# Sample differential attention: four heads on one 128-column array pass, or on four 32-column strips

## The reference, cut to what matters

```python
s = jnp.einsum('bqhcd,bshcd->bhcqs', q, k) * HEAD_DIM ** -0.5      # b: 8 batches, q: 16 frames, s: 528 keys
s = s + bias; s = where(visible, s, -inf)
p = softmax(s, axis=-1)
p = p[:, :, 0] - lam * p[:, :, 1]                                  # the two halves of a head
o = jnp.einsum('bhqs,bshv->bqhv', p, v)                            # v: 128 wide
o = _rmsnorm(o, g_subln) * (1.0 - lam_init)
```

## Time and profile before

| | |
|---|---|
| runs shown | 2597.21, 2597.66, 2604.88 us; median 2597.66 us |
| the profiled execution | 2597.61 us, of which the span from the first to the last instruction is 2595.2 us |
| PE busy | 2503.7 us (96% of the span), mean granted clock 0.986 |
| DVE, ACT, POOL busy | 1447.8 us (56%), 1033.3 us (40%), 266.0 us (10%) |
| chain that ended last | PE 81%, DVE 8%, issue 4%, ACT 3%, DMA 3% |

### The profile page before, as it was taken

How to read it: one execution, slowest core, us unless ns; L and a number is a source line. 1 busy time by engine, 2 the same in 40 slices (tenths; PEclk the granted TensorE clock), 3 DMA queues, 4 the chain that set the end, 5 groups by cost and what they waited for, 6 DMA issues and landing times.

```text
span 2595.2 us, 36227 instructions
## 1 busy us (share of the span) xinstructions
PE 2503.7 (96%) x13547; PEld 2155.1 (83%) x13547; DVE 1447.8 (56%) x2884; ACT 1033.3 (40%) x1801; POOL 266.0 (10%) x363
## 2 busy tenths in 40 slices
PE   7999999999989999999999999999999999999998
PEld 5999999878867677778778889989888889888887
DVE  4534444454355358887655348888876545444444
ACT  3322222233332136566424337777565523222221
POOL 1100000014200001110014300000100001000000
PEclk7999999999999999999999999999999999999999
DMA  6212121233355253333433462232311132322221
GB/s 223 82 66 82 66 82 65 102 126 119 109 160 168 68 174 95 112 106 92 160 114 102 149 190 70 85 98 77 98 53 45 49 139 68 135 98 97 98 91 71
DMA packets 169004, 271.29 MB, mean 105 GB/s; under 512 B 72096, under 2 KB 104384, under 8 KB 168832
## 3 DMA queue, kind: packets, MB, share of 16 engines
q0 software_dynamic: 43200, 167.29, 19.2%
q1 hardware_dynamic: 125632, 101.69, 12.3%
HBM read 235.21 MB, written 35.29 MB: 104 GB/s over the span
## 4 chain that ended last, share of the span: by engine, by line
PE 81%; DVE 8%; issue 4%; ACT 3%; DMA 3%; SPq 1%; DVEq 0%; ACTq 0%; POOL 0%
PE bank L1383 12%; PE bank L1384 12%; PE bank L1385 12%; PE bank L1400 6%; PE bank L1401 6%; PE bank L1402 6%; PE bank L1420 4%; PE bank L1422 4%; PE bank L1421 4%; PE bank L1510 3%; DVE w_lo L1971 2%; PE bank L1479 1%; PE bank L1645 1%; PE bank L1493 1%; PE bank L1480 1%
## 5 line engine op out<-in xcount | busy, mean ns | idle before, releaser
L1971 DVE TENSOR_TENSOR w_lo<-raw,w_hi 128x1024 fp32r<-128x1024 f32 x320 | 385.9, 1217 | 148.5 <-ACT w_hi L1685 148.0
L1383 PE MATMUL bank<-XTh_a,w_hi 128*128 128x320 f32 x1408 | 441.4, 313 | 7.2 <-DVE w_lo L1971 2.9
L1385 PE MATMUL bank<-XTh_a,w_lo 128*128 128x320 f32 x1408 | 436.9, 310 | 0.0
L1384 PE MATMUL bank<-XTl_a,w_hi 128*128 128x320 f32 x1408 | 436.9, 310 | 0.0
L1685 ACT ACTIVATE w_hi<-raw 128x1024 fp32r<-128x1024 f32 x320 | 331.5, 1047 | 229.2 <-PE bank L1422 127.3
L1400 PE MATMUL bank<-w_hi,hid_hi 128*128 128x512 f32 x792 | 317.4, 401 | 23.0 <-DVE X_b L2002 8.2
L1401 PE MATMUL bank<-w_lo,hid_hi 128*128 128x512 f32 x792 | 313.1, 395 | 0.0
L1402 PE MATMUL bank<-w_hi,hid_lo 128*128 128x512 f32 x792 | 311.1, 393 | 0.0
L1383 PE MATMUL bank<-XTh_b,w_hi 128*128 128x512 f32 x704 | 284.1, 404 | 0.0
L1384 PE MATMUL bank<-XTl_b,w_hi 128*128 128x512 f32 x704 | 279.0, 396 | 0.0
L1385 PE MATMUL bank<-XTh_b,w_lo 128*128 128x512 f32 x704 | 278.9, 396 | 0.0
(11 more groups left out here) (318 smaller groups left out, 4053.7 us busy)
## 6 DMA issues: line engine op xcount, KB each, us to landing
raw<-in_w_gate POOLq DMA_DIRECT2D x44, 1024.0 KB, 5.7
raw<-in_w_up POOLq DMA_DIRECT2D x44, 1024.0 KB, 5.7
raw<-in_w_down POOLq DMA_DIRECT2D x44, 1024.0 KB, 5.3
raw<-in_w_in POOLq DMA_DIRECT2D x16, 1024.0 KB, 5.4
s_k_in<-in_cache_diff_k SPq DMA_DIRECT2D x16, 512.0 KB, 3.8
s_v_in<-in_cache_diff_v SPq DMA_DIRECT2D x8, 1024.0 KB, 5.6
raw<-in_w_out POOLq DMA_DIRECT2D x8, 1024.0 KB, 5.4
q_rows_b<-q_scr SPq DMA_DIRECT2D x80, 64.0 KB, 2.1
```

Of the source, the lines that this page charges most:

```text
L1383: pe.matmul(out, hi[:, k], XTh[g][:, k, lo:up], start=(k == 0), stop=False)
L1384: pe.matmul(out, hi[:, k], XTl[g][:, k, lo:up], start=False, stop=False)
L1385: last = pe.matmul(out, low[:, k], XTh[g][:, k, lo:up], start=False, stop=(k == KD - 1))
L1971: dve.tensor_tensor(hilo(w_lo, u)[:, :, 0:width_of(u)], raw_part(u), hilo(w_hi, u)[:, :, 0:width_of(u)].bitcast(F32), ALU.subtract).then_i ...
```

## The change

The four heads get strips of 32 array columns, and with them 32 output partitions each. In `x_score` a head's stationary operand is only its own 32 columns of `qm` (now 128 columns wide, without the zero blocks), and its output is partitions `h*32` to `h*32+31`; the heads no longer add into one another. The values' matmuls take 32 columns of `s_pT` (16 queries and 16 columns that are zeroed once), write partitions `h*32` on, and the loop runs over key blocks outside and heads inside. ACT's copies into `s_pT` put each head's 16 columns at `h*32`; DVE copies 128 partitions x 128 columns in place of 16 x 512; the store of a batch is four transfers of 16 rows x 128 columns in place of one; the counts on its semaphore go with it.

```diff
--- before.py
+++ after.py
@@ -151,6 +151,7 @@
 ROUNDS = -(-SAMPLE_TOPK // 8)
 KT = PAST // P
 BATCH_PAIRS = DEC_BATCH // 2
+STRIP = P // DIFF_HEADS
 TAGS = ("n1a", "n1b", "n2a", "n2b", "n3a", "n3b")
 
 
@@ -1071,8 +1072,8 @@
                     idx_T = lay_i("s_idx_T", [P, 2, SAMPLE_KEYS])
                 v_in = lay_d("s_v_in", [P, 2, KT + 1, 512])
                 diff_T = lay_d("s_diff_T", [P, 2, DIFF_HEADS, SAMPLE_KEYS])
-                qm = lay_d("s_qm", [P, 2, 640])
-                o_batch = lay_d("s_o_batch", [DEC_SEQ, 2, 512])
+                qm = lay_d("s_qm", [P, 2, P])
+                o_batch = lay_d("s_o_batch", [P, 2, VD])
             with ExitStack() as stage:
                 def lay_e(name, shape, dt=F32):
                     return stage.enter_context(nc.sbuf_tensor(name, shape, dt))
@@ -1599,8 +1600,8 @@
                         part, cols = out_of(key)[:, 0:HALF], slice(n * HALF, (n + 1) * HALF)
                         if diff:
                             for h in range(DIFF_HEADS):
-                                last = pe.matmul(part, qm[:, b % 2, h * P:(h + 1) * P], diff_T[:, b % 2, h, cols], start=(h == 0),
-                                                 stop=(n == 0 and h == DIFF_HEADS - 1))
+                                last = pe.matmul(part[h * STRIP:(h + 1) * STRIP], qm[:, b % 2, h * STRIP:(h + 1) * STRIP],
+                                                 diff_T[:, b % 2, h, cols], start=True, stop=(n == 0))
                         else:
                             half = slice((b % 2) * HD, (b % 2 + 1) * HD)
                             pe.matmul(part, qd[half, b, :], dsa_T[half, (b // 2) % 2, cols], start=True, stop=False)
@@ -1639,11 +1640,11 @@
                     vacant(pe, key)
                     if diff:
                         pe.wait_ge(s_v_loaded[b % 2], 32 * (b // 2 + 1))
-                        for h in range(DIFF_HEADS):
-                            for k in range(KT + 1):
-                                part = slice(0, P if k < KT else DEC_SEQ)
-                                last = pe.matmul(out_of(key)[0:DEC_SEQ, h * VD:(h + 1) * VD],
-                                                 s_pT[part, u % 2, k, h * DEC_SEQ:(h + 1) * DEC_SEQ],
+                        for k in range(KT + 1):
+                            part = slice(0, P if k < KT else DEC_SEQ)
+                            for h in range(DIFF_HEADS):
+                                last = pe.matmul(out_of(key)[h * STRIP:(h + 1) * STRIP, 0:VD],
+                                                 s_pT[part, u % 2, k, h * STRIP:(h + 1) * STRIP],
                                                  v_in[part, b % 2, k, h * VD:(h + 1) * VD], start=(k == 0), stop=(k == KT))
                     else:
                         pe.wait_ge(s_dv_loaded[b % 4], 32 * (b // 4 + 1))
@@ -1934,15 +1935,19 @@
                     if u >= 2:
                         done(act, ("x_weigh", u - 2))
                     done(act, main)
-                    copied = act.activation(s_pT[:, u % 2, 0:KT, 0:width], out_of(main)[:, 0:KT * width].rearrange("p (k n) -> p k n", k=KT), ACT.Copy)
                     if diff:
-                        tail, key = out_of(main)[0:DEC_SEQ, KT * width:(KT + 1) * width], main
+                        if u < 2:
+                            act.wait_ge(s_zeroed, 2 + 1)
+                        strips = s_pT[:, u % 2].rearrange("p k (h n) -> p k h n", n=STRIP)
+                        src = out_of(main)[:, 0:(KT + 1) * width].rearrange("p (k h i) -> p k h i", k=KT + 1, i=DEC_SEQ)
+                        act.activation(strips[:, 0:KT, :, 0:DEC_SEQ], src[:, 0:KT], ACT.Copy)
+                        act.activation(strips[0:DEC_SEQ, KT, :, 0:DEC_SEQ], src[0:DEC_SEQ, KT], ACT.Copy).then_inc(frees(main), 1)
                     else:
-                        copied.then_inc(frees(main), 1)
+                        act.activation(s_pT[:, u % 2, 0:KT, 0:width], out_of(main)[:, 0:KT * width].rearrange("p (k n) -> p k n", k=KT), ACT.Copy
+                                       ).then_inc(frees(main), 1)
                         key = ("x_probs", u, 1)
                         done(act, key)
-                        tail = out_of(key)[0:DEC_SEQ, 0:P]
-                    act.activation(s_pT[0:DEC_SEQ, u % 2, KT, 0:width], tail, ACT.Copy).then_inc(frees(key), 1)
+                        act.activation(s_pT[0:DEC_SEQ, u % 2, KT, 0:width], out_of(key)[0:DEC_SEQ, 0:P], ACT.Copy).then_inc(frees(key), 1)
 
                 def x_norm(part):
                     if part == 0:
@@ -2398,8 +2403,8 @@
                     done(dve, key)
                     if diff:
                         if b >= 2:
-                            dve.wait_ge(s_batch_stored[b % 2], 16 * (b // 2))
-                        dve.tensor_copy(o_batch[:, b % 2], out_of(key)[0:DEC_SEQ, :]).then_inc(frees(key), 1)
+                            dve.wait_ge(s_batch_stored[b % 2], 16 * DIFF_HEADS * (b // 2))
+                        dve.tensor_copy(o_batch[:, b % 2], out_of(key)[:, 0:VD]).then_inc(frees(key), 1)
                     else:
                         dve.tensor_copy(oT_s[:, :, b, :], out_of(key)[0:HD, 0:P].rearrange("p (h i) -> p h i", i=DEC_SEQ)).then_inc(frees(key), 1)
 
@@ -2495,6 +2500,7 @@
                     pool.wait_ge(fence, 1)
                     pool.memset(qi[:], 0.0).then_inc(s_zeroed, 1)
                     pool.memset(qm[:], 0.0).then_inc(s_zeroed, 1)
+                    pool.memset(s_pT[:], 0.0).then_inc(s_zeroed, 1)
 
                 def x_norm(part):
                     if part == 1:
@@ -2732,12 +2738,14 @@
 
                 def x_o_store(b):
                     emptied(sp, ("x_weigh", b))
-                    sp.dma_start(o_scr[NP * P + b * DEC_SEQ:NP * P + (b + 1) * DEC_SEQ, 0:512], o_batch[:, b % 2, :]).then_inc(s_batch_stored[b % 2], 16)
+                    for h in range(DIFF_HEADS):
+                        sp.dma_start(o_scr[NP * P + b * DEC_SEQ:NP * P + (b + 1) * DEC_SEQ, h * VD:(h + 1) * VD],
+                                     o_batch[h * STRIP:h * STRIP + DEC_SEQ, b % 2, :]).then_inc(s_batch_stored[b % 2], 16)
 
                 def x_norm(part):
                     if part == 0:
                         for n in range(2):
-                            sp.wait_ge(s_batch_stored[n], 16 * (DEC_BATCH // 2))
+                            sp.wait_ge(s_batch_stored[n], 16 * DIFF_HEADS * (DEC_BATCH // 2))
                         sp.dma_start(s_rows[:], o_scr[NP * P:T, 0:512]).then_inc(s_rows_loaded, 16)
                     elif part == 2:
                         sp.wait_ge(s_onormed, 1)
```

## The result

| | before | after |
|---|---|---|
| median of the runs (lowest to highest) | 2598.5 us (2597.21 to 2604.88) | 2562.14 us (2559.83 to 2566.66) |
| the profiled execution, its span | 2597.61, 2595.2 us | 2561.53, 2559.7 us |

The direction was right, the size was not.

A forecast was written before the change was run, and what follows sets the result against it. PE was taken to bound the kernel, at 81% of the chain's span. From 2597.6 us, 22.1 came off for scores and values and 0.4 was added for stores and copy, giving 2576 us; range 2565 to 2596.

The forecast's parts named there:

- Between them stands what the order of passes allows: Score and value matmuls on PE: each head costs one pass and a 0.027 us load instead of two passes.
- all four strips at once: Rival, both matmul stages: scores 1.1 us, values 1.4 us, DVE's search takes some back; 2559 us, chance 0.08.
- The forecast terms: PE's two matmul stages per unit: scores 2.30 us instead of 3.56, value product 3.11 us instead of 5.18.
- The units that keep the gain: Scores keep 1.26 us in units 1 to 6, values 2.07 us in seven batches: 22.1 us.
- the gain is made and a wait takes it: Rival: late four-issue stores hold DVE's copies for batches 2 to 5, some 10 us lost; 2586 us, chance 0.08.
- the slack of a store at 0.2 us: Tightest store before DVE's copy two batches later: 7.1 us left, slowest landing 6.9 us, so it just fits.
- The give-back of DVE's search: In the rival of four strips at once, DVE's 4.4 us search outlasts the value product: 0.5 us back in five units.
- Unit 0 into the wait for keys, unit 7 into the stall: Unit 0's score gain goes into the 3.1 us keys wait; unit 7's gains lengthen the `s_hidden` stall to 7.4 us.
- Switches: Shape changes between matmuls, 0.10 us each: six of eight go per value product, -0.6 us a unit; scores gain one.
- Copy and stores: DVE's copy about 0.29 us; store issues 0.49 us each, +1.5 us of SP a unit; +0.4 us in the stall.
- No overlap: Rival, both matmul stages: strips run one after the other, values -0.58 us, scores +0.1; 2594 us, chance 0.22.
- a drain at each strip: Rival: each strip change costs 0.10 us, values +1.22, scores +0.8 us a unit; 2611 us; chance 0.10 including open loads.

The follow-up runs named there:

- the four stores: The kernel before, with only each batch's store split into four transfers of 128 columns: 2599.28 us, ratio to before 1.0002.
- two blocks in a row: The whole change, but the value product takes two key blocks of a head before the next head: 2562.89 us, ratio to before 0.9865.
- four blocks: The whole change, but the value product takes a head's four 128-row blocks in a row, all 16-row blocks last: 2565.78 us, ratio to before 0.9864.
- heads outside: The whole change, but the value product loops over heads outside and key blocks inside: 2586.30 us, ratio to before 0.9940.

## Why the prediction was right in sign and wrong in size

- **The failed step** is "Between them stands what the order of passes allows", and in it that only the next head's first pass may run beside a head's second. That the second pass of a head waits for the first was right. But the runs showed that a waiting pass doesn't hold the passes behind it: the first passes of all four heads run together and then their second ones, so eight passes take two slots of 109 ns (0.22 us), where the forecast had 4 x 0.137 = 0.55. Its load of 0.027 us was too long besides: the loads start 7 ns apart. The upper bound that the text itself named, all four strips at once, is what happened: 1.1 and 1.4 us stood there for the stages, 1.02 and 1.36 were measured. The forecast terms were 2.30 and 3.11. The chance of 0.08 for that case rested on "passes in order, two on one strip", which no row had shown.
- **The units that keep the gain** were right: six times the scores and seven times the values, 6 x 2.54 + 7 x 3.82 = 42.0 us. From the timeline, unit by unit: units 1 to 6 are shorter by 2.4, 6.3, 5.8, 3.1, 5.5 and 6.3 us, the stretch from unit 7's scores to unit 8's is the same (16.71 and 16.78), from unit 8's to unit 10's 7.7 shorter. With 1.6 from unit 0 that is 38.8; the 1.6 is no more than unit 0 differs by between before and the four stores (18.35 and 16.98 us), whose scores are the same.
- **What was lost** on the way is 4.6 us: 0.5 in unit 3 with a wait for keys, 3.3 in unit 4 with another and the lower clock behind it, and 0.8 in unit 5 by DVE's late copy of keys. Only the last is the mechanism of the rival "the gain is made and a wait takes it", which had late stores hold DVE; keys that land late in a shorter unit stood in no rival. The text expected no new wait of DVE for the stores of batches 0 to 2, and there were two, 0.91 us for batch 1's and 0.47 for batch 2's. It had the slack of a store at 0.2 us with a gain of 3.3 a unit; with 6.4 there was none. Another 4.1 us went in the rest of the kernel, 1704.7 to 1708.8, inside what that stretch varies by.
- **The give-back of DVE's search**, 0.5 us in five units of the last rival, did not come: unit 2 is shorter by the whole 6.3 us, with DVE busy 96% of it. That this rival's sum of 38.8 us is also the gain of the stretch is luck: it is 41.3 less the 2.5 of the give-back.
- **Unit 0 into the wait for keys, unit 7 into the stall**: right. The first wait grew by 2.3. The string from `x_new(7)` to `x_score(8)` stayed at 17.9 and 18.0 us (848.07 to 865.97; 816.17 to 834.14). That the wait came out at 7.6, beside 7.4 forecast, is luck: 4.1 + 6.36 = 10.5 was due, and 2.9 of it went ahead of it into a wait of 1.23 us for `s_dsa_in` and, behind that, into the lower clock (the value product 822.04 to 824.22, 2.18 us for 1.36, and the main stream's next matmuls).
- **Switches** were right: 789 to 1011 ns is a pass of 0.109 us and 0.11 for the change of shape. **Copy and stores** too: the copy takes 0.292 us (0.29 forecast), an issue 0.46 (0.49), and four stores alone change nothing.
- **No overlap, and a drain at each strip**, are refuted by the first four starts, 7 ns apart on four strips.

## What to carry to other kernels

Matmuls that use a quarter of the array's columns run four at a time if the queue has neighbours on different strips, and up to four passes in a row on one strip did no harm here; put the loop over strips inside. When such a change halves a unit, ask at once what the unit's transfers need: here the 2 MB of keys and values a unit became what units wait for, and moving each batch's store and the first two loads of values in the queue was worth another 18 us. A bound that excludes a gain should rest on a row that shows it; where none does, the chance of the far bound is not 0.08.

## What the runs showed of the hardware that was not expected

Passes on different column strips start 7 ns apart, with their weight loads, on the same rows. The starts fit a strip that holds one running pass and three waiting ones before the queue stops: with two blocks in a row all four strips run, with four blocks only a head's last four passes (of eight) run beside the next head's first four. A change of the stationary tile's shape between two heads (heads outside) left no overlap at that border.
